# Recurrent layer of a four-layer model: one minus the decay, an input of the scan, made by ScalarE behind its square root, not by VectorE

## The reference, cut to what matters

```python
def lru_mixer(h, w_in, conv_w, conv_b, wa, ba, wx, bx, a_param, w_out):
    u = h @ w_in.astype(h.dtype)
    xb, gate = u[..., :LRU_WIDTH], u[..., LRU_WIDTH:]
    xc = causal_depthwise_conv(xb, conv_w, conv_b)
    r = jax.nn.sigmoid(block_diag_linear(xc, wa, ba).astype(jnp.float32))
    i = jax.nn.sigmoid(block_diag_linear(xc, wx, bx).astype(jnp.float32))
    log_a = -LRU_C * r * jax.nn.softplus(-a_param.astype(jnp.float32))
    a = jnp.exp(log_a)
    mult = jnp.sqrt(-jnp.expm1(2.0 * log_a))
    bterm = mult * (i * xc.astype(jnp.float32))
    ...
    _, hs = lax.associative_scan(combine, (a, bterm), axis=1)   # hs[t] = a[t]*hs[t-1] + bterm[t]
    y = hs.astype(h.dtype) * jax.nn.silu(gate)
    return y @ w_out.astype(h.dtype)
```

## Time and profile before

| | |
|---|---|
| median of 3 runs | 2282.89 us (2282.76 to 2283.53) |
| the profiled execution | 2283.32 us, of it the span of the trace 2281.5 us |
| PE busy | 2258.5 us, 99% of the span |
| DVE busy / ACT busy | 1286.8 us (56%) / 819.9 us (36%) |
| recurrent layer's six groups | from about 65 to 213 us of the span |
| of 155.00 us from 60 to 215 us: PE / DVE / ACT busy | 150.26 / 127.62 / 111.52 us |

### The profile page before, as it was taken

How to read it: one execution, slowest core, us unless ns; L and a number is a source line. 1 busy time by engine, 2 the same in 40 slices (tenths; PEclk the granted TensorE clock), 3 DMA queues, 4 the chain that set the end, 5 groups by cost and what they waited for, 6 DMA issues and landing times.

```text
span 2281.5 us, 27680 instructions
## 1 busy us (share of the span) xinstructions
PE 2258.5 (99%) x10088; PEld 1848.7 (81%) x10098; DVE 1286.8 (56%) x1832; ACT 819.9 (36%) x1125; POOL 1.4 (0%) x6
## 2 busy tenths in 40 slices
PE   9999999999999999999999999999999999999997
PEld 7788877778888888888888888888888888888886
DVE  7878785658556335555453545655335555553545
ACT  5776463545233212233221223234222233222222
POOL 0000000000000000000000000000000000000000
PEclk9999999999999999999999999999999999999998
DMA  4333212213222322232323223222222233223322
GB/s 171 95 108 102 89 50 74 74 61 111 74 74 74 111 95 99 94 100 93 102 85 109 92 93 102 74 83 81 98 98 95 85 106 102 93 93 102 101 93 74
DMA packets 59508, 211.63 MB, mean 93 GB/s; under 512 B 6736, under 2 KB 7120, under 8 KB 59280
## 3 DMA queue, kind: packets, MB, share of 16 engines
q1 hardware_dynamic: 58464, 207.78, 27.7%
q0 software_dynamic: 224, 1.31, 0.2%
q10 hardware_dynamic: 720, 1.16, 0.2%
HBM read 208.14 MB, written 2.10 MB: 92 GB/s over the span
## 4 chain that ended last, share of the span: by engine, by line
PE 86%; DVE 2%; ACT 1%; issue 0%; DVEq 0%; ACTq 0%
PE bank L619 25%; PE bank L620 25%; PE bank L621 25%; PE bank L779 2%; PE bank L616 2%; PE bank L614 2%; PE bank L615 2%; PE bank L819 2%; PE bank L808 1%; PE bank L766 1%; PE bank L748 0%; PE bank L749 0%; PE bank L830 0%; DVE y_lo L1575 0%; ACT arena L1120 0%
## 5 line engine op out<-in xcount | busy, mean ns | idle before, releaser
L1269 DVE TENSOR_TENSOR w_lo<-w_raw,w_hi 128x1024 fp32r<-128x1024 f32 x387 | 467.7, 1224 | 773.5 <-ACT w_hi L901 772.6
L901 ACT ACTIVATE w_hi<-w_raw 128x1024 fp32r<-128x1024 f32 x387 | 404.1, 1057 | 944.6 <-PE bank L621 915.6
L619 PE MATMUL bank<-h_hi,w_hi 128*128 128x512 f32 x1792 | 703.3, 392 | 4.8 <-DVE arena L1304 2.0
L620 PE MATMUL bank<-h_lo,w_hi 128*128 128x512 f32 x1792 | 698.4, 390 | 0.0
L621 PE MATMUL bank<-h_hi,w_lo 128*128 128x512 f32 x1792 | 698.3, 390 | 0.0
L619 PE MATMUL bank<-y_hi,w_hi 128*128 128x512 f32 x1056 | 411.0, 389 | 1.6 <-DVE w_lo L1269 1.3
L621 PE MATMUL bank<-y_hi,w_lo 128*128 128x512 f32 x1056 | 410.8, 389 | 0.0
L620 PE MATMUL bank<-y_lo,w_hi 128*128 128x512 f32 x1056 | 410.8, 389 | 0.0
L619 PEld LDWEIGHTS bank<-h_hi,w_hi 128*128 128x128 f32 x1792 | 337.1, 188 | 78.0 <-DVE w_lo L1269 4.3
L620 PEld LDWEIGHTS bank<-h_lo,w_hi 128*128 128x128 f32 x1792 | 337.2, 188 | 71.1 <-issue 1.7
L621 PEld LDWEIGHTS bank<-h_hi,w_lo 128*128 128x128 f32 x1792 | 337.1, 188 | 70.3
(11 more groups left out here) (204 smaller groups left out, 1404.5 us busy)
## 6 DMA issues: line engine op xcount, KB each, us to landing
w_raw<-in_stream SPq DMA_DIRECT2D x389, 512.0 KB, 3.3
out_t<-x SPq DMA_DIRECT2D x8, 256.0 KB, 2.2
x<-in_x_t ACTq DMA_DIRECT2D x4, 256.0 KB, 6.9
x<-in_x_t SPq DMA_DIRECT2D x4, 256.0 KB, 8.5
arena<-in_consts POOLq DMA_DIRECT2D x1, 1024.0 KB, 5.3
w_raw<-in_stream SPq DMA_DIRECT2D x2, 256.0 KB, 4.0
arena<-in_positions POOLq DMA_DIRECT2D x1, 256.0 KB, 6.0
vec_t<-in_vecs ACTq DMA_DIRECT2D x1, 112.5 KB, 3.8
```

The lines of the kernel that those rows point to most:

```text
L619: pe.matmul(out, w_hi[:, slot, w], a_h, start=first, stop=False)
L620: pe.matmul(out, w_hi[:, slot, w], a_l, start=False, stop=False)
L901: A.activation(w_hi[:, slot, :], w_raw[:, slot, :], ACT.Copy).then_inc(hi_ready, 1)
L1269: V.tensor_tensor(w_lo[:, slot, :], w_raw[:, slot, :], w_hi[:, slot, :].bitcast(F32), ALU.subtract).then_inc(lo_ready, 1)
```

## The change

ACT computes the decay: `Identity(-1 * d + 1)` in place on `g_d`, 128x1024, right behind its square root, the one being read from a column of a tile of ones. DVE's L1469 and the wait ahead of it go. The counters are adjusted: `input_gate` adds 6 to `act_out` and 3 to `vec`.

```diff
@@ INCS
-    "input_gate": {"act_out": 5, "vec": 4},
+    "input_gate": {"act_out": 6, "vec": 3},
@@ input_gate on ScalarE
                 act.wait_ge(vec, T.value("vec", 2))
                 A.activation(g_t, g_t, ACT.Sqrt, scale=-1.0).then_inc(act_out, 1)
+                A.activation(g_d, g_d, ACT.Identity, scale=-1.0, bias=ones[:, 0:1]).then_inc(act_out, 1)
@@ input_gate on VectorE
                 V.scalar_tensor_tensor(out=g_t, in0=g_d, scalar=2.0, in1=g_d, op0=ALU.subtract,
                                        op1=ALU.mult).then_inc(vec, 1)
                 V.tensor_tensor(g_i, g_i, xc[:, blk:blk + 2, :], ALU.mult).then_inc(vec, 1)
-                got(2)
-                V.tensor_scalar(g_d, g_d, -1.0, 1.0, ALU.mult, ALU.add).then_inc(vec, 1)
```

## The result

The changed kernel takes 2288.24 us (median of 19 runs, 2286.04 to 2288.88), the kernel before 2282.73 in the same comparison (19 runs, 2280.97 to 2283.57): 5.5 us more, ratio 1.0025, 95% interval 1.0019 to 1.0031. It is slower, by a quarter of a per cent.

What follows compares the result with a forecast made beforehand. A chain through DVE and ACT sets each group's end; PE, 99% busy, meets it only where late. Five delays of 1.055 us plus 0.56 make 5.84 on the 2282.89 median: 2288.7 us, range 2287.0 to 2290.0.

Steps and rivals of the forecast that it cites:

- What goes brings nothing in five groups: Removing DVE's 0.687 us L1469 gains nothing where DVE waits 0.34 us for ACT's copy anyway; only the sixth gains.
- The price of 1.055 per group: New ACT instruction between root and chunk copy delays what follows by 1.055 us in five groups, bounds 0.93 to 1.17.
- The delays add up: The ACT-DVE chain is closed from group to group, so five delays of 1.055 us sum to 5.275.
- The sixth group, 0.56: In the sixth group the scan waits for the new ACT instruction and starts 0.56 us later.
- The sum, 5.84: Whole delay over six groups: 5 x 1.055 + 0.56 = 5.84 us, bounds 5.0 to 6.45.
- The signs: Expected in the new profile: idle 2.1 us before w_lo, PE's waits some 10 us, last near 219.0, sixth scan 0.56 later.
- The clock: Around the edited steps the granted clock is 1.00, its upper level of 2.4 GHz, so it plays no part.
- PE's single waits: PE's waits, group by group: 1.18 to 2.2 us at 109.33, 0.31 to 1.4 at 170.81, 1.31 to 2.4 at 213.17.
- Rival 1: DVE binds and gets relief of 0.69 us per group, 4.1 in all: 2278.8 us, not slower; chance 0.08.
- Rival 2: PE holds the chain in the fourth cycle, whose 1.055 us delay is lost: 4.8 more, 2287.7 us; chance 0.08.
- Rival 3: New ACT instruction brings a 1.28 us table load on the chain six times: 13.5 more, 2296.4 us; chance 0.02.
- A reading: Five 0.34 us waits of w_lo for ACT's copy called the bulk of 8 waits, 5.7 us in all, one 3.6 elsewhere.

Runs made afterwards that it cites:

- e1: Kernel before without DVE's L1469 and nothing in its place: median 2281.64 us, ratio 0.9997.
- e2: Changed kernel with a second Identity of the same size behind the first, on the dead tile g_r: 2292.87 us, ratio 1.0052 to the kernel before.
- e8: Kernel before with the decay moved to ACT in the sixth group alone: 2283.17 us, ratio 1.0004.
- e10: Kernel before with the product L1467 moved ahead of L1461, into DVE's idle time: 2280.95 us, ratio 0.9995.
- e4: Changed kernel with the first chunk copy moved ahead of ACT's square root: 2278.75 us, ratio 0.9985 to the kernel before.
- e5: Kernel before, decay still on DVE, with the first chunk copy moved ahead of ACT's square root: 2279.98 us, ratio 0.9990.
- e3: Kernel before with the decay on ACT in five groups, behind both chunk copies; sixth group left on DVE: 2281.79 us, ratio 1.0000.
- e9: Changed kernel, first chunk copy and product L1467 moved earlier, Identity counted with the closing product's step in five groups: 2274.70 us, ratio 0.9973 to the kernel before.

## Why the prediction was right

It gave 2288.7 with 2287.0 to 2290.0; measured 2288.24. By its steps:

- *What goes brings nothing in five groups.* Right: e1 gains 0.49 us, all of it in the sixth group, forecast 0.5 with its expectation.
- *The price of 1.055 per group.* The instruction is 1.135 us long, not 1.155, and moves the copy by 1.04 (106.14 to 107.18). The groups grew by 1.03 to 1.05. Mis-sized by 0.015, 0.08 in all.
- *The delays add up.* Right, and shown by e2: 11.95 against 12.0.
- *The sixth group, 0.56.* From d to scan it was 205.25 - 200.94 = 4.31 and is 209.83 - 204.98 = 4.85: 0.54. Alone (e8): 0.56.
- *The sum, 5.84.* Measured 5.74 in the stretch. The medians differ by 5.5, within what the spread of the runs allows.
- *The signs.* Most held: idle before `w_lo` 1.98 (forecast 2.1), last wait of PE 2.28 (2.4), a new small one of 0.27 at 187.97 (0.49), the scan of the sixth group 0.54 later behind d (0.56). Two did not. PE's waits in the stretch were to rise to some 10 us and rose to 7.2; the next two items say where the rest went. And the last wait was to end near 219.0, with an end before 218 as a sign of being wrong: it ends at 217.74. The stretch starts 1.17 us earlier in this profile, so it is 218.91 on the clock of the profile before. The sign was set in absolute time, where the opening counts too; in time from the first d it held.
- *The clock.* The prediction gave it no part, as its granted share was 1.00 before. In the changed kernel it fell twice in the stretch, and PE lost 3.3 us by it (next item). Added to the 2.5 us by which its waits grew (4.7 to 7.2), that is PE's share of the 5.74. It is no cost on top, nor the cause: neither DVE nor ACT has a wait for PE between 60 and 225 us of the changed kernel, and e2, where it fell at one place only, was on its forecast. That the forecast held in spite of it was in part luck: the fall behind the last wait, from where PE runs without a wait to the end of the stretch, did not come. What it would have cost there was not measured.
- *PE's single waits.* Partly wrong. I had the one at 109.33 grow to 2.2 and the one at 170.81 to 1.4. They are 0.59 and none. PE was late itself: behind its waits of 2.15 and 1.88 us it did some eight matmuls each at nearly half its pace (below) and lost 1.7 and 1.6 us, which came out of waits that it would have had. So PE's column was wrong in two groups and the end right, since the chain through ACT and DVE sets it; at the last wait PE still had 2.3 us in hand.
- *Rival 1.* False by e1 and e10. The Trainium skill (Perfetto Trace Analysis, Optimizing Scalar/DVE Operations) says that offloading to ScalarE may make sense where DVE is saturated. DVE was 82% busy here and still had idle time exactly behind the instruction that was taken away. With the chunk copy out of the way (e4 against e5) the same offloading does bring 1.2 us. *Rival 2* false by e2. *Rival 3* false: there is no table load with L1054, in its six places.
- *A reading.* The five waits of 0.34 us are the bulk of the 8 waits of `w_lo` by number only; of the 5.7 us they are 1.7, and 3.6 are the one that lies elsewhere. The sum does not use it.

## What to carry to other kernels

Work moved to a less busy engine costs what it delays in that engine's queue: look at the first instruction behind it and who waits for that, not at the busy shares. A chain that goes back and forth between two engines is shortened by putting independent work into their waits (here the chunk copy and the product, 6 us), and lengthened by whatever is put between its links. A wait for "all that the other engine has done so far" makes a moved instruction a link of the chain, even where nobody needs its result yet.

## What the runs showed of the hardware

**PE's pace after a wait.** After the wait of 2.15 us in the changed kernel eight of PE's matmuls come every 0.43 us, then they come every 0.23 again. The first of them:

```profile
99.57 0.50 PE L619 MATMUL bank<-h_hi,w_hi 128*128 128x512 f32 x1 [2.15 <-DVE w_lo L1270]
99.91 0.58 PE L620 MATMUL bank<-h_lo,w_hi 128*128 128x512 f32 x1
100.29 0.63 PE L621 MATMUL bank<-h_hi,w_lo 128*128 128x512 f32 x1
100.71 0.63 PE L619 MATMUL bank<-h_hi,w_hi 128*128 128x512 f32 x1
101.14 0.63 PE L620 MATMUL bank<-h_lo,w_hi 128*128 128x512 f32 x1
```

The granted clock of this stretch is 0.66 on the mean (99 to 104 us), that is partly the lower level of 1.2 GHz, and 0.66 again from 137 to 142 us, behind the wait of 1.88:

```profile
99.00:104.00 5.00, 4.43 (x12) 3.51 (x13) 2.96 (x4) 4.78 (x6) 0.00 (x0) 0.66 0.58 178
```

Behind the wait of 2.28 at 217.74 the clock stays at 1.00. In e2 it is 0.66 behind a wait of 3.25 us (110.5 to 115.5 us) and 1.00 behind waits of 2.81 and 3.33. So the length of the wait alone does not tell. What does, these runs leave open.

**The opening, and the spread of the runs.** PE's first long wait ends at 7.3 to 7.6 us in every profile, and behind it between none and 14 matmuls come at the slow pace, 0.2 us more each: 14 in the profile of before (2.8 us in all), 9 in that after (1.7), none in e2, e3, e8 and e9. The pace is read from their starts: the granted clock from 7 to 12 us is 0.66 in the profile after, but 1.00 in that of before, with 11 matmuls in the 5 us. The difference of 1.1 us is nearly all of the 1.17 by which the stretch starts earlier after. It is not the only spread: in the four profiles with none the stretch starts between 70.97 and 71.85. The 2.8 us are as much as the spread between runs of one kernel (2280.97 to 2283.57), though only the profiled runs show the opening, and the cause of that spread was not tested. It says nothing of an edit; a difference of a few microseconds between two profiles of this kernel should be read from a point behind it.
